# Expert rows of a mixture-of-experts layer scattered to (choice, token) order instead of stored by tile and gathered back

## The reference

```
scores = sigmoid(h @ w_router);  sel = scores + b_router        # 16 experts in 4 groups
best = the group with the largest sum of its two best sel
idx  = the two experts with the largest sel inside that group   # TOP_K = 2
w    = scores[idx] / sum(scores[idx])
out  = sum over the two choices of w * (silu(h @ w_gate[e]) * (h @ w_up[e])) @ w_down[e]
x    = x + gt2 * out                                            # gt2: a gate per channel
```

## Time and profile before

| | |
|---|---|
| median of 3 runs | 1787.61 us (1786.41 to 1787.65) |
| the profiled execution | 1783.93 us, its span 1782.1 us |
| TensorE busy | 1626.1 us, 91% of the span |
| VectorE busy | 1035.8 us, 58% |
| ScalarE busy | 824.1 us, 46% |
| GpSimd busy | 233.2 us, 13% |
| expert tiles of layer 0 | 617.1 to 874.4 us of the span |
| expert tiles of layer 1 | 1482.5 to 1739.0 us |

### The profile page before, as it was taken

The page is one execution under the profiler, slowest core; times in us unless marked ns, Lnnn a source line. Parts: engine busy times, 40 slices in busy tenths (PEclk is TensorE's granted clock), DMA queues, the critical chain, the costliest instruction groups (busy, mean ns, idle before and its releaser), DMA issues. The chain is left out here.

```text
span 1782.1 us, 22085 instructions
## 1 busy us (share of the span) xinstructions
PE 1626.1 (91%) x8260; PEld 1207.9 (68%) x8260; DVE 1035.8 (58%) x1853; ACT 824.1 (46%) x1501; POOL 233.2 (13%) x282
## 2 busy tenths in 40 slices
PE   3999999999999799999669999999999977999990
PEld 0777777777887567676357777777778765676760
DVE  2476655356555767676366666444556566676743
ACT  4534553445323356666364455444551333666640
POOL 1000000011100112222210000001110001222213
PEclk9999999999999899999889999999999988999995
DMA  9531235344645899999745320553453647999976
GB/s 353 192 125 42 72 107 185 116 122 152 236 161 214 299 368 413 413 413 413 298 119 194 143 72 23 195 173 108 145 169 125 213 177 277 414 413 413 413 296 192
DMA packets 106778, 399.41 MB, mean 224 GB/s; under 512 B 12704, under 2 KB 12768, under 8 KB 106160
## 3 DMA queue, kind: packets, MB, share of 16 engines
q1 hardware_dynamic: 73152, 266.37, 39.8%
q0 software_dynamic: 33376, 129.01, 20.3%
q10 hardware_dynamic: 144, 2.62, 0.4%
HBM read 347.03 MB, written 49.45 MB: 222 GB/s over the span
## 5 line engine op out<-in xcount | busy, mean ns | idle before, releaser
L1144 DVE TENSOR_TENSOR lo<-raw,hi 128x1024 fp32r<-128x1024 f32 x298 | 353.0, 1221 | 129.9 <-ACT hi L800 128.3
L1762 PE MATMUL ps<-hi,hT_hi 128*128 128x512 f32 x960 | 395.1, 412 | 18.9 <-DVE hT_lo L1254 15.9
L1764 PE MATMUL ps<-hi,hT_lo 128*128 128x512 f32 x960 | 378.6, 394 | 0.0
L1763 PE MATMUL ps<-lo,hT_hi 128*128 128x512 f32 x960 | 377.5, 393 | 0.0
L800 ACT ACTIVATE hi<-raw 128x1024 fp32r<-128x1024 f32 x298 | 299.3, 1055 | 138.2 <-DMA raw<-w_stream 131.8
L1762 PEld LDWEIGHTS ps<-hi,hT_hi 128*128 128x128 f32 x960 | 182.4, 190 | 78.2 <-issue 26.3
L1764 PEld LDWEIGHTS ps<-hi,hT_lo 128*128 128x128 f32 x960 | 182.2, 190 | 41.0
L1763 PEld LDWEIGHTS ps<-lo,hT_hi 128*128 128x128 f32 x960 | 183.1, 191 | 33.2
L2089 PE MATMUL ps<-over,xT 128*128 128x512 f32 x288 | 127.2, 594 | 0.5 <-DMA over<-w_moe 0.5
L1762 PE MATMUL ps<-hi,xT_hi 128*128 128x512 f32 x256 | 103.7, 405 | 3.7 <-DVE xT_lo L1608 3.7
L1764 PE MATMUL ps<-hi,xT_lo 128*128 128x512 f32 x256 | 100.8, 394 | 0.0
(11 more groups left out here) (282 smaller groups left out, 2687.4 us busy)
## 6 DMA issues: line engine op xcount, KB each, us to landing
raw<-w_moe SPq DMA_DIRECT2D x192, 512.0 KB, 11.0
raw<-w_stream SPq DMA_DIRECT2D x112, 512.0 KB, 4.0
over<-w_moe SPq DMA_DIRECT2D x108, 512.0 KB, 12.9
raw_m<-w_stream SPq DMA_DIRECT2D x70, 512.0 KB, 5.4
ye_d<-ysb POOLq DMA_DIRECT2D x50, 512.0 KB, 7.1
bias_na<-na_bias POOLq DMA_DIRECT2D x32, 384.0 KB, 3.3
sg<-sg_d POOLq DMA_DIRECT2D x8, 1280.0 KB, 9.9
raw_p<-w_stream SPq DMA_DIRECT2D x16, 512.0 KB, 15.9
```

Of the source, the lines that this page charges most:

```text
L1144: dve.tensor_tensor(lo[s][:], raw[s][:], hi[s][:].bitcast(F32), ALU.subtract).then_inc(is_lo.sem, 1)
L1762: pe.matmul(out, w_hi, m_hi, start=first, stop=False)
L1763: pe.matmul(out, w_hi, m_lo, start=False, stop=False)
L1764: return pe.matmul(out, w_lo, m_hi, start=False, stop=last)
```

## The change

TensorE works out a second table beside `w_slot`: `row_i`, for every slot the row j * 640 + token of (choice, token) that it holds, by ten more small matmuls on `row_t`. `store_rows` becomes an indirect DMA that scatters the 128 rows of `ysb` by `row_i` into `ye_d`, which now has 1280 rows in order of choice and token. Unused slots get an index beyond the bounds, in `inv_i` and in `row_i`, so that they are neither gathered nor stored. The ten gathers on GpSimd go away. SyncE issues ten plain loads instead (`load_back`), Y1 and Y2 of each token tile, behind the first six weight units of layer 1, and at the end of the kernel. VectorE adds Y2 to Y1 for all five token tiles. `y_out` is stored from SyncE's queue. The diff without the removed and added declarations:

```diff
@@ SyncE
+                def load_back(l):
+                    for b in range(2):
+                        sp.wait_ge(y_stored[b].sem, y_stored[b].at(l, half[b] - 1))
+                    for t in range(NT):
+                        for j, dst in enumerate((Y1[t], Y2[t])):
+                            r0 = (j * NT + t) * P
+                            sp.dma_start(dst[:], ye_d[r0:r0 + P, :]).then_inc(gathered[t].sem, 16)
+
                 for u in range(NU):
                     s = uslot[u]
                     sp.wait_ge(used[s].sem, used[s].at(l, u // SLOTS - 1))
                     sp.dma_start(raw[s][:], w_stream[l, u]).then_inc(loaded[s].sem, 16)
+                    if l >= 1 and u == SLOTS - 1:
+                        load_back(l - 1)
...
+            load_back(DEPTH - 1)
+            for t in range(NT):
+                sp.wait_ge(x_ready.sem, x_ready.at(DEPTH - 1, t))
+                sp.dma_start(y_out[:, t, :], x[:, t, :]).then_inc(s_out, 16)
+            sp.wait_ge(s_out, 16 * NT)
@@ GpSimd
                     po.indirect_dma_start(xg[n % 2][:], None, h2_d,
-                                          bass.IndirectOffsetOnAxis(inv_i[:, XD_COL[n]:XD_COL[n] + 1], 0)
+                                          bass.IndirectOffsetOnAxis(inv_i[:, XD_COL[n]:XD_COL[n] + 1], 0),
+                                          bounds_check=NT * P - 1, oob_is_err=False
                                           ).then_inc(xg_loaded[n % 2].sem, 16)
...
-                    po.dma_start(ye_d[XD_COL[n] * P:(XD_COL[n] + 1) * P, :], ysb[n % 2][:]).then_inc(y_stored[n % 2].sem, 16)
+                    if n == 0:
+                        po.wait_ge(ws_ready.sem, ws_ready.at(l, 0))
+                    po.indirect_dma_start(ye_d, bass.IndirectOffsetOnAxis(row_i[:, XD_COL[n]:XD_COL[n] + 1], 0),
+                                          ysb[n % 2][:], None, bounds_check=2 * NT * P - 1,
+                                          oob_is_err=False).then_inc(y_stored[n % 2].sem, 16)
...
-                po.wait_ge(slot_ready.sem, slot_ready.at(l, 0))
-                for b in range(2):
-                    po.wait_ge(y_stored[b].sem, y_stored[b].at(l, half[b] - 1))
-                def choice(t, j):
-                    dst = Y2[t] if (t, j) == (0, 1) else Y1[t]
-                    if t >= 1 and j == 1:
-                        po.wait_ge(gathered[t].sem, gathered[t].at(l, 0))
-                    po.indirect_dma_start(dst[:], None, ye_d, bass.IndirectOffsetOnAxis(slot_i[:, j, t:t + 1], 0),
-                                          compute_op=ALU.add if t >= 1 and j == 1 else ALU.bypass
-                                          ).then_inc(gathered[t].sem, 16)
-
-                for t, j in ((0, 0), (1, 0), (0, 1), (2, 0), (3, 0), (1, 1), (4, 0), (2, 1), (3, 1), (4, 1)):
-                    choice(t, j)
-
-            for t in range(NT):
-                po.wait_ge(x_ready.sem, x_ready.at(DEPTH - 1, t))
-                po.dma_start(y_out[:, t, :], x[:, t, :]).then_inc(s_out, 16)
-            po.wait_ge(s_out, 16 * NT)
@@ VectorE
                     dve.wait_ge(gathered[t].sem, gathered[t].at(l, 1))
-                    if t == 0:
-                        after(chained(dve.tensor_tensor(Y1[0][:], Y1[0][:], Y2[0][:], ALU.add)))
+                    after(chained(dve.tensor_tensor(Y1[t][:], Y1[t][:], Y2[t][:], ALU.add)))
...
-                dve.tensor_copy(inv_i[:], ps[:, 4, 0:MOE_TILES]).then_inc(inv_ready.sem, 1)
+                TS(inv_i[:], ps[:, 4, 0:MOE_TILES], float(NT * P), None, ALU.add).then_inc(inv_ready.sem, 1)
...
-                dve.tensor_copy(slot_i[:], slot_f[:]).then_inc(slot_ready.sem, 1)
...
+                TT(row_t[:], one_t[:], tok[:].unsqueeze(2).to_broadcast([P, 2 * NT, MOE_TILES]), ALU.mult)
...
+                        TS(row_i[:], ps[:, 4, 2 * MOE_TILES:3 * MOE_TILES], float(2 * NT * P), None, ALU.add)
@@ TensorE, slot_weights
+                    for i in range(2 * NT):
+                        ins = pe.matmul(ps[:, 4, 2 * MOE_TILES:3 * MOE_TILES], one_p[:, i, :], row_t[:, i, :],
+                                        start=(i == 0), stop=(i == 2 * NT - 1))
                     ins.then_inc(ws_done.sem, 1)
@@ host
-    tok_in = np.arange(NT * P, dtype=f).reshape(NT, P).T
+    tok_in = (np.arange(2 * NT * P, dtype=f) - 2 * NT * P).reshape(2 * NT, P).T
```

More of the change, by code:

```diff
@@ L188, in program @@
         rc = at("rc", [P, NRC], BF16)
-        tok = at("tok", [P, NT], F32)
+        tok = at("tok", [P, 2 * NT], F32)
         junk_off = top[0]
@@ L230, in program @@
         slot_f = at("slot_f", [P, 2, NT], F32)
-        slot_i = at("slot_i", [P, 2, NT], I32)
         n_tiles = at("n_tiles", [P, N_EXP], F32)
@@ L235, in program @@
         base1 = at("base1", [P, N_EXP], F32)
+        ecmp_off = top[0]
         ecmp = at("ecmp", [P, N_OVER, N_EXP], F32)
+        row_i = nc.alloc_sbuf_tensor_at("row_i", [P, MOE_TILES], I32, offset=ecmp_off)
         w_slot = at("w_slot", [P, MOE_TILES], F32)
@@ L302, in program @@
         w_part = in_junk("w_part", [P, 3, 2 * NT], F16, 1.625)
+        row_t = in_junk("row_t", [P, 2 * NT, MOE_TILES], F16, 1)
         w_rest = in_junk("w_rest", [P, 2 * NT], F32, 1.75)
@@ L319, in program @@
         sg_d = nc.dram_tensor("sg_d", [len(GATES), NT, P, 512], F32, kind="Internal").ap()
-        ye_d = nc.dram_tensor("ye_d", [MOE_TILES * P, D], F32, kind="Internal").ap()
+        ye_d = nc.dram_tensor("ye_d", [2 * NT * P, D], F32, kind="Internal").ap()
         ps = ctx.enter_context(nc.psum_tensor("ps", [P, 8, 512], F32))
@@ L440, in program @@
         inv_ready = Signal("inv_ready", 1)
-        slot_ready = Signal("slot_ready", 1)
         etab_ready = Signal("etab_ready", 1)
@@ L1588, in _ @@
                     js = slice(j * NT, (j + 1) * NT)
-                    TT(tok_t[:, js, :], one_t[:, js, :], tok[:].unsqueeze(2).to_broadcast([P, NT, MOE_TILES]), ALU.mult)
+                    TT(tok_t[:, js, :], one_t[:, js, :], tok[:, NT:2 * NT].unsqueeze(2).to_broadcast([P, NT, MOE_TILES]),
+                       ALU.mult)
                 for j in range(2):
```

## The result

The changed kernel takes 1769.82 us, the median of 4 runs (1767.62 to 1772.16), against 1787.63 us for the kernel before on the same chip: a ratio of 0.9894 (0.9872 to 0.9917). The profiled execution took 1772.16 us, its span 1770.4.

The account below looks back on a forecast made before the run. TensorE was taken to bound the expert stage, leaving gains in the tails behind both layers. Head -2.9, final tail -4.6, matmuls +0.5, overflow weights -0.5 sum to -7.5 us: 1787.6 becomes 1780.1, range 1774 to 1786.

Parts of the forecast that it names:

- VectorE's start, -5.1 and -4.5: Behind layers 0 and 1, plain loads in place of gathers let VectorE start 5.1 and 4.5 us earlier.
- Four adds, 0.3 + 0.96 + 0.96 in the head: In layer 1's head, VectorE's new adds of 1.23 us each come through only in part, 2.2 us in sum.
- The last add of the final tail: Behind layer 1, VectorE's chain of adds takes 18.5 us and ends at 1766.4, 4.3 us earlier.
- Ten matmuls, 0.25 us per layer: The new table's matmuls, 0.025 us each, lie on TensorE's path: 0.25 us per layer, 0.5 in all.
- Scatters cost nothing: In the expert stage, row stores as indirect DMAs on GpSimd cost nothing as long as a tile lasts 10 us.
- rival B: In the expert stage, GpSimd's scatters hold back VectorE: 23 us more, less 7.5, giving 1804 us; chance 0.08.
- 0.3 us for the quicker issue and landing: At the kernel's end, y_out stores from SyncE's idle queue issue and land faster, gaining 0.3 us.
- The stage is TensorE's, and fewer bytes in it are worth at most that 0.5 us.: In the expert tiles DMA follows TensorE, so less traffic saves only layer 1's 0.5 us wait for overflow weights.
- Rival C: DMA sets the pace somewhere in the expert stage; a tenth of 38 us per layer gives 1772 us; chance 0.08.
- The first gather: zero taken: At each layer's first gather, no change counted, with bounds from 0.7 us better to 1.4 worse per layer.
- the removed copy of slot_i was off the path: nothing: Ahead of the expert tiles, removing VectorE's copy of slot_i changes the time by nothing.
- Rival A: The tails gain, but slow checked indirect DMAs (2.37 us) and bare adds eat it: +0.7 us, 1788; chance 0.16.

Follow-up runs that it names:

- e2: The changed kernel with only the y_out stores and the wait for them moved back from SyncE's queue to GpSimd's: 1780.77 us, ratio 0.9954.
- e1: The kernel before with only its y_out stores and the wait for them moved from GpSimd's queue to SyncE's: 1781.85 us, ratio 0.9957.
- e6: The changed kernel with four short VectorE operations ahead of each layer's first split, and overflow weights waiting for the first gather: 1767.18 us, ratio 0.9872.
- e7: The changed kernel with unused slots gathering token 0 again, without a check of bounds; the scatter stays checked: 1775.17 us, ratio 0.9929.

## Why the prediction was right in direction and wrong in size

- **VectorE's start, -5.1 and -4.5.** Right: -5.5 and -4.8. Gathers on GpSimd were replaced by loads that VectorE has 5.03 and 4.85 us from issue, for the 4.6 taken. The fit of the Trainium skill, "DMA: Bandwidth & Descriptors", "Anatomy of one DMA", which the prediction set beside it, is given there for DMAs issued from GpSimd, and these go out on SyncE; no term rests on it.
- **Four adds, 0.3 + 0.96 + 0.96 in the head.** Right in the steps that a trace shows: 0.37 us at tile 0 for 0.3, and 0.97 from tile 2 to tile 3 (e2) for 0.96. That the whole head comes to +2.3 for +2.2 is in part luck, since profiles of one head differ by 4 us with the clock. The last add of the final tail is right: -4.8 for -4.3.
- **Ten matmuls, 0.25 us per layer.** Right: from the second tile's transposes to the third's, 9.19 us before and 9.45 after in layer 0, 8.75 and 9.01 in layer 1.
- **Scatters cost nothing, rival B.** Right: 1.0 us each, splits unchanged. They were even quicker than the 1.8 us taken; so are the checked gathers, at a median of 1124 ns against 1800.
- **Wrong, the largest: "0.3 us for the quicker issue and landing".** The step treated what lies behind the last landing as fixed. It is 7.6 us in before (1774.5 to 1782.1), and the earlier trace rows against the span of 1782.1 showed it: the chain of waits was followed to the last store and not to the end of the span. The stretch gave 8.4 us. Undone in the changed kernel (e2) it costs 7.6 of them, done alone in the old one (e1) it gives the 8.4 in that stretch.
- **Wrong: "The stage is TensorE's, and fewer bytes in it are worth at most that 0.5 us."** They were worth 5.6 us with the matmuls' 0.5 in it, so 6.1. The step read TensorE's waits only and set aside one of them as VectorE's: the 2.3 us for hid, which stand in layer 0's slow third tile. One level further, the waits of VectorE and ScalarE, led to a DMA of weights. Rival C was this mechanism with a chance of 0.08. Its size (7.6 us) came near only because it took a tenth for an example. Its sign, tiles shorter than 255 us, didn't come: from the first tile's matmuls to the last `ysb`, layer 0 went from 257.3 to 255.5, with the 1.6 us lost to the clock inside it.
- **Wrong: "The first gather: zero taken"**, and with it "the removed copy of slot_i was off the path: nothing". The two stretches got 6.0 us longer, 4.0 of them at the gather and 2.0 in the first tile. The bounds of 0.7 better to 1.4 worse per layer considered the instruction's own length, and that held: 1.0 to 1.1 us more where it is long. They left out what starts beside it, VectorE's split and, in layer 1, six loads of weights. With both put right (e6) gather to transposes is 4.4 us in both layers (before: 4.3 and 4.7). The 2.0 us of the first tile are no part of the gather, and no run shows whether the change causes them: the lower clock came in seven of the nine profiles of the changed kernel and its variants, and in none of the three of the kernel before and e1. Rival A's sign, an indirect instruction above 1.5 us at the first gather, came (2.12 and 2.00), but not by A's mechanism: e7's gather has no check and takes 2.05 us in layer 1, where the split starts first, and 1.02 in layer 0, where it doesn't. The check has a small part in the order: without it the gather is issued 0.07 to 0.08 us earlier behind `inv_i`, and in layer 0, where the split also comes 0.07 us later, the gather stays ahead of it.

The difference to the forecast of the stretches is -8.1 (end) - 5.6 (expert tiles) + 6.0 (first gathers) - 1.1 (all others) = -8.8 us: -16.35 against -7.5. The medians say -17.8. Two of the three errors nearly cancelled, by luck, and the DRAIN carried the time out of the range.

What stays open: what sets the length of GpSimd's DRAIN, what gives layer 1's expert tiles their 1.6 us, how layer 1's 3.5 us at the gather divide between the split and the weights, and why the clock fell in one first tile and not in another.

## What to carry to other kernels

Follow the chain to the end of the span: what an engine does after its last useful instruction is part of the time, and which engine issues the last stores decides whether GpSimd's closing DRAIN is bare. When a busy engine has a short wait in a stage that DMA fills, follow the releaser's own waits until one ends at a transfer, before the bytes are called free. Where VectorE and GpSimd start within 0.2 us of each other, the removal of a tiny operation can turn their order and cost more than it saves; that is a reason to fix the order by hand. And before a stretch with TensorE in it is credited to an edit, compare its granted clock in a second profile: here it moved one first tile by 1.6 us and one head by up to 4.

## What the runs showed of the hardware beyond that

- GpSimd's closing DRAIN took 7.26 us in both profiles of before, 7.99 in the changed kernel and six of its variants, 6.44 in e2 and 13.0 in e1; TensorE's took 3.7, ScalarE's 0.7, VectorE's 1.3 and SyncE's 0.007 to 0.12.
- A scatter with a check of bounds takes GpSimd 0.97 to 1.03 us, however many of its rows are left out.
- A scatter that stores nothing completes 2.1 us from its issue.
- A first gather that starts 0.03 to 0.15 us behind a VectorE split takes 2.0 to 2.1 us instead of 1.0, in ten cases of eleven; in the eleventh it took 1.06 and the split 1.29 instead of 1.22.
